# Eleven taps of a causal depthwise convolution moved from TensorE to ScalarE and GpSimd, and the attention values of the sample rows gathered in one pair of PSUM banks

## What is computed

```python
def mixer_block(x, conv_past, ...):
    z = rms_norm(x, norm_g) @ w_in                      # 1024 -> 2048 columns: u, v, a, b
    gm_u, gm_v, cv_a, cv_b = jnp.split(z, [...], axis=-1)
    u = jax.nn.gelu(gm_u)
    v = layer_norm(jax.nn.gelu(gm_v), gm_ln_g, gm_ln_b)
    a_out = (u * chunk_spatial_mix(v, gm_ws, gm_bs))
    glu = cv_a * jax.nn.sigmoid(cv_b)                   # 512 channels
    full = jnp.concatenate([conv_past, glu], axis=1)
    conv = depthwise_conv(full, conv_w) + conv_b        # 31 taps for each channel
    b_out = jax.nn.silu(layer_norm(conv, cv_ln_g, cv_ln_b))
    y = x + jnp.concatenate([a_out, b_out], axis=-1) @ w_out

def memory_cross_attention(x, mem_k, mem_v, ...):       # sample tokens: keys and values of their own
    p = jax.nn.softmax(scores * XA_HEAD_DIM ** -0.5)
    o = jnp.einsum('nhtm,nmhd->nthd', p, mem_v)
    return x + o @ wo
```

## Time and profile before

| | |
|---|---|
| median of 3 runs | 686.86 us (686.58 to 687.76) |
| time of the profiled execution | 687.92 us |
| span of the profiled execution, first to last instruction | 686.0 us |
| busy: TensorE, VectorE, ScalarE, GpSimd | 595.5, 318.0, 197.9, 78.8 us |
| mean granted TensorE clock | 0.939 of 2.4 GHz |
| moved by DMA | 181.56 MB, mean 265 GB/s |

### The profile page before, as it was taken

The page is one execution under the profiler, slowest core; times in us unless marked ns, Lnnn a source line. Parts: engine busy times, 40 slices in busy tenths (PEclk is TensorE's granted clock), DMA queues, the critical chain, the costliest instruction groups (busy, mean ns, idle before and its releaser), DMA issues.

```text
span 686.0 us, 11980 instructions
## 1 busy us (share of the span) xinstructions
PE 595.5 (87%) x4915; PEld 467.8 (68%) x4915; DVE 318.0 (46%) x626; ACT 197.9 (29%) x337; POOL 78.8 (11%) x129
## 2 busy tenths in 40 slices
PE   5899999889999999999989966989989987489810
PEld 5899996567899999985788853555655664246400
DVE  4669787879644464788403174121121121011147
ACT  6422323154834344444012241111111111011132
POOL 0000000700002200010212101111111111110100
PEclk9999999999999999999989965999999999689965
DMA  8852210325544314679696396999999999999663
GB/s 328 315 222 103 83 63 3 125 83 180 188 149 168 123 63 134 250 305 419 233 392 262 131 406 231 364 421 418 420 417 421 419 421 420 419 420 415 259 266 127
DMA packets 35651, 181.56 MB, mean 265 GB/s; under 512 B 8943, under 2 KB 10127, under 8 KB 16765
## 3 DMA queue, kind: packets, MB, share of 16 engines
q1 hardware_dynamic: 26733, 165.62, 61.5%
q0 software_dynamic: 5600, 12.76, 4.9%
q10 hardware_dynamic: 3264, 2.42, 1.1%
HBM read 174.94 MB, written 15.61 MB: 278 GB/s over the span
## 4 chain that ended last, share of the span: by engine, by line
PE 68%; SPq 14%; DVE 7%; DMA 6%; issue 3%; ACT 2%; ACTq 0%; DVEq 0%; POOLq 0%
PE ps L1708 13%; PE ps L1710 13%; PE ps L1709 13%; SPq L626 9%; PE ps L2123 8%; PE ps L2151 4%; DMA w<-exp_w 4%; SPq L635 4%; PE ps L1829 4%; PE ps L1704 3%; PE ps L1909 2%; PE ps L1930 2%; PE ps L1971 1%; DVE x L1656 1%; DVE x L1658 1%
## 5 line engine op out<-in xcount | busy, mean ns | idle before, releaser
L1708 PE MATMUL ps<-xH,w_h 128*128 128x260 f32 x480 | 138.8, 289 | 2.3 <-DVE glu L1182 2.0
L1710 PE MATMUL ps<-xL,w_h 128*128 128x260 f32 x480 | 136.2, 284 | 0.0
L1709 PE MATMUL ps<-xH,w_l 128*128 128x260 f32 x480 | 136.2, 284 | 0.0
L2123 PE MATMUL ps<-w,xeT 128*64 128x256 f32 (+2 forms) x1024 | 120.7, 406 | 13.5 <-DMA w<-exp_w 12.2
L2123 PEld LDWEIGHTS ps<-w,xeT 128*64 128x64 f32 (+2 forms) x1024 | 81.8, 145 | 57.2 <-issue 29.4
L1708 PEld LDWEIGHTS ps<-xH,w_h 128*128 128x128 f32 x480 | 91.2, 190 | 6.3 <-issue 5.7
L1709 PEld LDWEIGHTS ps<-xH,w_l 128*128 128x128 f32 x480 | 91.2, 190 | 0.2
L1710 PEld LDWEIGHTS ps<-xL,w_h 128*128 128x128 f32 x480 | 91.1, 190 | 0.0
L1057 DVE TENSOR_TENSOR w_l<-raw,w_h 128x2048 fp32r<-128x2048 f32 x27 | 61.8, 2289 | 27.6 <-ACT w_h L739 27.4
L2151 PE MATMUL ps<-w,aT 128*64 128x512 f32 (+2 forms) x256 | 60.3, 627 | 16.1 <-DVE aT L1621 12.2
L739 ACT ACTIVATE w_h<-raw 128x2048 fp32r<-128x2048 f32 x27 | 51.6, 1910 | 21.9 <-PE ps L1710 19.2
(11 more groups left out here) (351 smaller groups left out, 859.5 us busy)
## 6 DMA issues: line engine op xcount, KB each, us to landing
w<-exp_w SPq DMA_DIRECT2D x96, 1024.0 KB, 22.9
raw<-weights SPq DMA_DIRECT2D x27, 1024.0 KB, 4.8
raw<-caches SPq DMA_DIRECT2D x16, 1024.0 KB, 7.8
qb<-q_rows POOLq DMA_DIRECT2D x4, 1024.0 KB, 5.6
yr<-y_rows SPq DMA_DIRECT2D x4, 1024.0 KB, 7.8
xT<-x_turned SPq DMA_DIRECT2D x4, 520.0 KB, 6.9
raw<-x_prompt SPq DMA_DIRECT2D x4, 512.0 KB, 12.0
x_rows<-x ACTq DMA_DIRECT2D x4, 512.0 KB
```

The costliest lines, as they stand in the source:

```text
L1708: pe.matmul(out, h1, h2, start=start, stop=False)
L1709: pe.matmul(out, l1, h2, start=False, stop=False)
L1710: return pe.matmul(out, h1, l2, start=False, stop=stop)
L2123: last = pe.matmul((mm[0][half, j, 0:FF], ta[1][half, 0:FF])[h], xeT[j][:, k, half], w13[s][:, h, k, :], start=k == 0, stop=k == KT_D - 1)
```

## The change

Taps 9 to 19 leave TensorE. For each of them and each group ScalarE multiplies 512 columns of `glu` by the tap's weight (44 instructions; those of tap 9 go straight into `tap_sum`, the other 40 into one of two buffers `product`), and GpSimd adds the 40 products to `tap_sum`. Four products stand ahead of ScalarE's own work of each block m = 4 to 14. TensorE keeps taps 20 to 30 and adds two parts ahead of the last, VectorE's and `tap_sum`. VectorE's own taps are now all inside the loop. The normalisation of `v` becomes a SCALAR_TENSOR_TENSOR that has the 1/std as a second tensor and is mixed with the memory's low parts; the 8 sample rows of `v` are scaled and shifted by VectorE. `token_norms` moves into block 2. Some stores share semaphores.

For the sample values the weights are padded: `s_own` holds for each token and head 32 columns of which only those of its own group are not zero (GpSimd writes the zeros, VectorE the rest in two copies), so that both groups add up in the same two banks, with two copies out of PSUM in place of four and 8 matmuls for `so` in place of 16. One half of the product with `wo` is split around the values, and two products of the router move up.

```diff
+POOL_TAPS = 11
+PE_FIRST = V_TAPS + POOL_TAPS
+PE_TAPS = TAPS - PE_FIRST
+PRODUCTS = [(k, c) for pair in ((0, 1), (2, 3)) for k in range(V_TAPS, PE_FIRST) for c in pair]
+PRODUCTS_AT = {m: 4 for m in range(4, 15)}
...
-            + ["ss", "sp", "or00", "or01", "or10", "or11", "so", ...
+            + ["ss", "sp", "or0", "or1", "so", ...
...
+        tap_sum = at("tap_sum", [P, 4, SEQ], F32, kT_at)
+        product = [at(f"product{i}", [P, SEQ], F32, v_at + 2 * PE_TAPS * BAND * 4 + 4 * SEQ * i) for i in range(2)]
+        s_own = at("s_own", [P, 2, 2, R // 2, 2, BAND // 2], F32, cl_at + 4096)
...
+            def products(count):
+                for _ in range(count):
+                    k, c = PRODUCTS[products_n[0]]
+                    products_n[0] += 1
+                    act.wait_ge(glu_ready, c + 1)
+                    if k == V_TAPS:
+                        dst = tap_sum[:, c, :]
+                    else:
+                        if sums_n[0] >= 2:
+                            act.wait_ge(product_added, sums_n[0] - 1)
+                        dst = product[sums_n[0] % 2][:]
+                        sums_n[0] += 1
+                    act.activation(dst, glu[:, c, k:k + SEQ], ACT.Copy, scale=cols_b[:, k, c:c + 1]).then_inc(product_made, 1)
...
                 for m in (2 * n, 2 * n + 1):
+                    products(PRODUCTS_AT.get(m, 0))
...
-            PART_AT = {4: 3, 5: 4, 6: 4, 7: 3, 8: 2, 9: 3, 10: 3, 11: 3, 14: 3}
+            PART_AT = {4: 3, 5: 4, 6: 4, 7: 3, 8: 4, 9: 4, 10: 4, 11: 4, 14: 2, 15: 4}
...
+            def normalised(j):
+                n_t = TILES[j][1]
+                for h in range(HEADS):
+                    row = (v_tok[:, j, :] if j < 4 else v_s[0:n_t])[:, h * P:(h + 1) * P]
+                    last = dve.scalar_tensor_tensor(row, row, mv[0:n_t, j, h, 0:1], mv[0:n_t, j, h, 1:2].broadcast_to([n_t, P]),
+                                                    ALU.subtract, ALU.mult)
+                return last
+            dve.tensor_scalar(mv[:, :, :, 1], mv[:, :, :, 1], EPS, None, ALU.add).then_inc(v_mean, 1)
+            memory_low(0)
+            memory_low(1)
             dve.wait_ge(v_root, 1)
             link(dve.reciprocal(mv[:, :, :, 1], mv[:, :, :, 1]))
-                    last = dve.tensor_scalar(row, row, mv[0:n_t, j, h, 0:1], mv[0:n_t, j, h, 1:2], ALU.subtract, ALU.mult)
+            for j in range(2):
+                normalised(j).then_inc(v_norm, 1)
+            memory_low(2)
+            for j in range(2, 4):
+                normalised(j).then_inc(v_norm, 1)
+            memory_low(3)
+            dve.wait_ge(consts_in, 16 * 6)
+            link(normalised(4))
+            link(dve.tensor_tensor(v_s[0:NS], v_s[0:NS], ln_g[0:NS], ALU.mult))
+            dve.tensor_tensor(v_s[0:NS], v_s[0:NS], ln_b[0:NS], ALU.add).then_inc(v_s_ready, 1)
...
-            dve.tensor_copy(s_pT[:].rearrange("p t r -> p (t r)"), src[:, 0:2 * R]).then_inc(tv_used, 1)
+            for g in range(2):
+                last = dve.tensor_copy(s_own[:, :, g, :, g, :], probs_of[:, :, g])
+            last.then_inc(tv_used, 1)
             residual(3, 0)
-            for g in range(2):
-                for b in range(2):
-                    src = take(f"or{g}{b}")
-                    dve.tensor_copy(o_s[g][:, 512 * b:512 * b + 512], src).then_inc(tv_used, 1)
+            for b in range(2):
+                src = take(f"or{b}")
+                dve.tensor_copy(o_s[:, 512 * b:512 * b + 512], src).then_inc(tv_used, 1)
...
-                project("w_in", m, xH, xL)
-                if m == 2:
-                    pe.wait_ge(dve_made, 1)
-                    token_norms()
+                project("w_in", m, xH, xL, (lambda k: token_norms() if k == 5 else None) if m == 2 else None)
...
-                for k in range(V_TAPS, TAPS):
+                for k in range(PE_FIRST, TAPS):
...
                         pe.wait_ge(part_done, 4 * V_TAPS)
-                        for r in range(4):
...
+                        pe.wait_ge(product_added, len(PRODUCTS) - 4)
+                        for part in (conv, tap_sum):
+                            for r in range(4):
...
-            half_of_wo(3, 0)
+            half_of_wo(3, 0, range(4))
             pe.wait_ge(tv_used, TV_AT["sp"] + 1)
...
+            half_of_wo(3, 0, range(4, 8))
...
-            for g in range(2):
-                for k in range(8):
-                    last = pe.matmul(out[:, k, 4 * g:4 * g + 4], o_s[g][:, k * P:(k + 1) * P], ident[:, 0::BAND],
+            for k in range(8):
+                last = pe.matmul(out[:, k, :], o_s[:, k * P:(k + 1) * P], one_row, start=True, stop=True)
             last.then_inc(tv_ready, 1)
+            for k in EARLY:
+                half_of_logits(k, 0)
...
+            for i, (k, c) in enumerate(PRODUCTS):
+                if k == V_TAPS:
+                    continue
+                pool.wait_ge(product_made, i + 1)
+                if c in last_of:
+                    pool.wait_ge(product_added, last_of[c])
+                pool.tensor_tensor(tap_sum[:, c, :], tap_sum[:, c, :], product[added % 2][:], ALU.add).then_inc(product_added, 1)
+                added += 1
+                last_of[c] = added
```

More of the change, by code:

```diff
@@ L43 @@
 V_TAPS = 9
-PE_TAPS = TAPS - V_TAPS
+POOL_TAPS = 11
[3 more added lines that the diff above has]
+PRODUCTS_AT = {m: 4 for m in range(4, 15)}
+assert sum(PRODUCTS_AT.values()) == len(PRODUCTS)
 MEM = 256
@@ L412, in trunk_kernel @@
         part_done = sem("part_done")
+        product_made = sem("product_made")
+        product_added = sem("product_added")
         conv_out = sem("conv_out")
@@ L1203, in _, with memory_low @@
                     part_taps(PART_AT.get(m, 0))
-            dve.tensor_scalar(mv[:, :, :, 1], mv[:, :, :, 1], EPS, None, ALU.add).then_inc(v_mean, 1)
-            part_taps(2)
-            for i in range(4):
+            def memory_low(i):
                 src = take(f"mem{i}").rearrange("p (k t) -> p k t", k=2)
@@ L1828, in conv_taps @@
                         for c in range(4):
-                            last = pe.matmul(out[r // 2][c * BAND:(c + 1) * BAND, r % 2, :], dw[c // 2][rows, c % 2, k - V_TAPS, :],
-                                             glu[rows, c, k:k + SEQ], start=k == V_TAPS, stop=k == TAPS - 1)
+                            last = pe.matmul(out[r // 2][c * BAND:(c + 1) * BAND, r % 2, :], dw[c // 2][rows, c % 2, k - PE_FIRST, :],
+                                             glu[rows, c, k:k + SEQ], start=k == PE_FIRST, stop=k == TAPS - 1)
                         if k == TAPS - 1 and r % 2:
@@ L1947, in _, with half_of_wo @@
             values(3)
-            def half_of_wo(k, b):
+            def half_of_wo(k, b, steps=range(8)):
                 n = W_AT[("wo", k // 2)]
@@ L1957, in half_of_wo @@
                 tok = slice(b * HT, (b + 1) * HT)
-                for kk in range(8):
+                for kk in steps:
                     if (k, b) == (0, 0):
@@ L2012, in logits_of @@
+            def logits_of(k):
+                for b in range(2):
+                    if b or k not in EARLY:
+                        last = half_of_logits(k, b)
                 if k == 7:
                     last.then_inc(ta_ready, 1)
-            pe.wait_ge(tv_used, TV_AT["or11"] + 1)
+            pe.wait_ge(tv_used, TV_AT["or1"] + 1)
             out = open_tv("so")[:, 0:8 * NS].rearrange("p (k s) -> p k s", k=8)
-            for g in range(2):
-                for k in range(8):
-                    last = pe.matmul(out[:, k, 4 * g:4 * g + 4], o_s[g][:, k * P:(k + 1) * P], ident[:, 0::BAND],
-                                     start=True, stop=True)
+            one_row = ident[:].rearrange("p (j g m) -> p g j m", g=2, m=BAND // 2)[:, :, :, 0]
```

117 lines of the change are left out of this document (60 added, 57 removed).

## The result

The changed kernel takes 702.22 us (median of 4 runs, 700.21 to 703.13) against 686.76 us of the kernel before on the same chip (686.58 to 687.76). The ratio is 1.0212, with a 95% interval of 1.0188 to 1.0236. The prediction was 694 us with a range of 670 to 702: the direction and the likeliest case were right, the loss was twice the size given, and the time lies 0.2 us outside the range. The profiled execution took 702.33 us.

A forecast was written before the change was run, and what follows sets the result against it. TensorE bounded most of the projection and the convolution, transfers the end; VectorE, held by GpSimd, would delay the memory products. 7.0 + 1.0 (clock) - 1.0 (sample values) = +7 us on 687.92 gives 694.9, by the median 694 us; range 670 to 702.

The forecast's parts named there:

- the likeliest case: Full hold of VectorE's two-SBUF-tensor instructions by GpSimd's additions: 694 us, its own range 688 to 702, chance 0.56.
- The hold between two-tensor instructions and GpSimd: Input projection: VectorE instructions with two SBUF tensors stand still during GpSimd's 40 additions, 1.1 us each, 44 us before cover.
- Rival 1: Projection: no hold between two-tensor instructions and GpSimd; memory products 14.9 us earlier, 671 us (668 to 675); chance 0.27.
- Rival 2: Projection: a hold mostly covered by VectorE's waits and PSUM work; `v_mean` near 118, 680 to 688 us; chance 0.13.
- Rival 3: Projection: no hold, but ScalarE becomes late with its products, stretching blocks by 1 to 3 us; 674 us; chance 0.04.
- VectorE needs 61.5 + 44 - 20 = 85.5 us: Projection: VectorE's work plus hold less cover, where it had 70 us; `v_mean` at about 124.6 (117 to 133).
- the cover: Projection: VectorE work that can lie beside GpSimd's additions, 23.3 us, of which all but 3 us is used.
- The sign that the prediction gave for its own case: Profile after: a 128x512 VectorE tap with median near 0.75 us and longest 1.7 to 2 us says hold.
- I take 20 us: Behind the projection: `v_mean` to ScalarE's root of `m_ss`, 25.8 us before, now 20 (18 to 21.6); root at 144.6.
- Clock +1.0: After TensorE idles some 15 us in pieces, its clock can be at 1.2 GHz; 1.0 us added.
- Token norms: Early projection: `token_norms` in the middle of block 2 removes block 3's 1.95 us wait for VectorE; 1.9 us saved.
- Sample values: At the sample values: `so` falls from 3.86 to 1.93 us, less longer waits; -1.0 us in all (0 to -2).

## Why the prediction was right, and where its size was off

**The hold between two-tensor instructions and GpSimd** was the step on which all rested, and it is right. The earlier trace rows leaned to it, showed it for another form. The additions as fills give 678.9, as additions 702.2: 23.3 us, the same as the distance of `v_mean` in the two traces (108.96 and 132.22). The Trainium skill, "SBUF — State Buffer", Who interferes with whom, says that GpSimd instructions which read SBUF exclude VectorE's two-input ones and that such which only write don't; the fills and copies agree with both halves. The longest tap, 1.07 us over its 0.746 beside additions of 1.27, is not far from the whole instruction of which the prediction speaks.

**Rival 1** (no hold, 671) fell. Its working was also too low: without hold the kernel takes 678.5 to 679.9, not 668 to 675. It took the convolution's end for the next limit; in fact `m_mean` at the end of VectorE's row holds ScalarE until 128, and TensorE waits 6.7 us for it. **Rival 2** (`v_mean` near 118, 680 to 688) fell too: VectorE's idle time took only some 5 of the 28.5 us of hold. **Rival 3** (ScalarE late) is not seen in the changed kernel, where VectorE's idle time from 39.1 us to `v_mean` is 4.8, of which only some 0.7 is not for TensorE; it appears only with split additions.

**"VectorE needs 61.5 + 44 - 20 = 85.5 us"** is the step that failed: it needed 93.3. Of these 60.0 are work (61.5 taken), 28.5 are hold (44 - 20 = 24 taken) and 4.8 are idle time, a term that the sum put at nothing: 4.2 of them are three waits for TensorE (0.70, 1.18 and 2.27 us), the two longer ones at the last two blocks. So `v_mean` came at 132.22 and not at 124.6, +7.6, near the upper bound of 133 that the text worked out for 40 additions at 1.3 us. In the hold, the price of one meeting was near the mark and the cover was too large. A tap stood 0.80 us at the median and 1.07 at most, where 1.1 was taken; 40 x 1.07 - 28.5 leaves at most 14 us of cover (an estimate), where 20 were taken. And the work that the text let lie beside GpSimd included instructions with two SBUF tensors, the two small groups that it left out. The larger one, in the changed kernel and with fills:

```profile
L1162 DVE TENSOR_TENSOR conv_s<-conv_s,cols 128x248 f32<-128x248 f32 x4 | 5.6, 1400 | 0.1
...
L1162 DVE TENSOR_TENSOR conv_s<-conv_s,cols 128x248 f32<-128x248 f32 x4 | 2.5, 620 | 0.1
```

With `dw` (3.5 us against 2.1) and the small copy `conv_s<-glu` (2.7 against 0.7) these are 6.5 of the 28.5 us.

The sign that the prediction gave for its own case, a tap with a median near 0.75 and a longest of 1.7 to 2 us, was half right: the longest is 1.82, the median 1.55. And it took GpSimd's additions to keep their 1.3 us, as in the earlier trace rows; in fact they are held as well (median 1.71).

**"I take 20 us" from `v_mean` to the root** measured 18.9 (151.15 - 132.22), and root to first product 1.55 for 2.0. So the first memory product is at 152.70, +13.1 in place of +7.0.

**Clock +1.0** measured 1.9 behind the idle piece of 6.8 us. Inside the projection the lower clock costs nothing that can be told: VectorE sets the pace there. TensorE's waits in the projection are 14.8 us (12 to 17 expected), but only 6.8 of them are for VectorE's `zt`; the others are for blocks of `v` that ScalarE or VectorE has not yet made ready or taken. **Token norms** -1.9 was right (-1.96 at the first memory product of the kernel with all taps on TensorE, where the other moves of that edit are in the number too; VectorE takes its first block at 26.50 in the changed kernel where it was 28.80). **Sample values** -1.0: `so` takes 1.95 us behind a wait of 1.72, both as said (1.93, 1.8), and the lag falls from 15.4 us ahead of the values (the turn of their scores starts at 343.46 against 328.09) to 14.6 at `xL`, -0.8.

The steps add up to 13.1 + 1.9 = 15.0 us at `vsT`, to 15.4 ahead of the sample values and to 14.6 at `xL`, on the profiled execution, where I had 7. The medians are 15.5 apart, since the profiled execution of before lies 1.2 us above its median and that of the changed kernel 0.1. The range was worked out with the right bound: with `v_mean` at 132.6 to 133 the sum gives 702.0 to 702.4. So the 0.2 us by which the median passed it say little (the four runs lie between 700.21 and 703.13); what was wrong is that the case at the upper bound was held to be the extreme and 85.5 the likely one.

## What to carry to other kernels

An engine whose row has room can still be the wrong place for work, if its instructions lock another engine out: price GpSimd instructions that read SBUF at what they take from VectorE, here on average 0.2 us for one of 0.6 to 0.7 us and 0.7 to 0.8 us for one of 1.1 to 1.3, and compare the sum with VectorE's idle time in that stage (10 us here). With holds of 8 to 10 us, below it, `v_mean` moved by 1.3 to 3.2 us; between 14 and 28.5 us of hold it moved by all that was added and more (6.7 to 23.3). The version with five added taps in short pieces gains 1.1%, of which the rest of the edit gives 0.5% without any tap moved. When a limit moves, look at what is queued last on the slow engine: a two-element `m_mean` behind 20 unrelated instructions cost 6.8 us of idle TensorE and 1.9 of clock, of which moving it gave back 4.3, because the next thing in VectorE's row then came last.

## What the runs showed of the hardware that I had not expected

The hold is not proportional to GpSimd's time. Per instruction VectorE stood 0.71 us (40 additions of 1.27), 0.70 (20 of the same), 0.82 (40 of `glu` without waits between, shortest 1.09), 0.24, 0.22 and 0.21 (40, 40 and 80 of 0.72) and 0.20 (40 copies of 0.61). These are averages over meetings and misses. A single meeting cost a tap up to 1.07 us beside additions of 1.27 and up to 0.49 or 0.55 beside those of 0.72 (one half in place of each addition, and two), some 0.2 us less than the length. How often a GpSimd instruction of a given length meets one of VectorE was not tried by itself.

A one-tensor TENSOR_SCALAR of 512 columns was held as well where additions were dense (0.48 alone, 1.10 on average; in the changed kernel its four met nothing and kept 0.48), and GpSimd is held just as VectorE is: an addition has a median of 1.71 us in place of 1.27, a longest of 3.68. Fills of GpSimd, even of 0.96 us, hold nothing.
